# Moving the weight slots and the low halves by 16 to 64 bytes in a four-layer decoder trunk

## The reference

```
layer 0, 3:  q, f, v, g = split(h @ w_in, 4)          # w_in 1024 x 4096
             gated linear recurrence in chunks of 64, 8 heads of 128; RMS norm; * silu(g)
layer 1:     h @ w_in                                  # w_in 1024 x 10240
             three dilated-window attentions (128,1), (512,4), (2048,16), 16 heads of 64,
             QK norm and ALiBi, merged by their softmax denominators; * silu(g)
layer 2:     u, v, g = split(h @ w_in, 3)              # w_in 1024 x 3072
             y = gelu(u) * (causal 128x128 mix of layer_norm(gelu(v)) + b_s) * silu(g)
every layer: x = x + y @ w_out                         # w_out 1024 x 1024
```

## Time and profile before

| | |
|---|---|
| median of 3 runs | 1348.52 us (1348.16 to 1348.88) |
| span of the profiled execution | 1346.8 us; the 1.7 us to the median lie around it |
| PE busy | 1339.1 us, 99% |
| PE weight loads busy | 1118.0 us, 83% (beside the matmuls) |
| DVE / ACT / POOL busy | 923.1 us / 687.2 us / 145.3 us |
| HBM traffic | 83 GB/s over the span |

### The profile page before, as it was taken

One profiled execution on the slowest core, in us unless ns is written; L12 is line 12 of the kernel. 1 busy time (PEld: TensorE's weight loads), 2 busy tenths in 40 slices (PEclk: granted clock), 3 DMA queues, 4 the chain that ended last, 5 costly groups with the idle time before them and its releaser, 6 DMA issues.

```text
span 1346.8 us, 22178 instructions
## 1 busy us (share of the span) xinstructions
PE 1339.1 (99%) x8759; PEld 1118.0 (83%) x8759; DVE 923.1 (69%) x1659; ACT 687.2 (51%) x1226; POOL 145.3 (11%) x224
## 2 busy tenths in 40 slices
PE   9999999999999999999999999999999999999999
PEld 8888888888888888888888887788888888888887
DVE  7867778564767576666676676865657577777782
ACT  6445555353655565656565656553434335454550
POOL 2422333000000000000000000000000022332220
DMA  6322233423222222222223131332333322232221
GB/s 194 95 80 79 64 94 95 118 79 91 66 79 79 79 79 79 79 79 79 79 68 90 48 92 50 105 93 71 94 94 94 110 76 83 63 93 76 84 64 63
DMA packets 211688, 113.62 MB, mean 84 GB/s; under 512 B 3743, under 2 KB 209889, under 8 KB 211586
## 3 DMA queue, kind: packets, MB, share of 16 engines
q1 hardware_dynamic: 211202, 112.02, 28.9%
q0 software_dynamic: 384, 0.20, 0.1%
HBM read 110.10 MB, written 2.10 MB: 83 GB/s over the span
## 4 chain that ended last, share of the span: by engine, by line
PE 96%; DVE 2%; ACT 1%; issue 1%; DMA 0%; SPq 0%; ACTq 0%; DVEq 0%
PE ps L647 39%; PE ps L662 38%; PE scores L662 4%; PE ps L1088 2%; PE ps L1072 2%; PE ps L1028 2%; PE ps L881 1%; PE scores L1056 1%; PE ps L1056 1%; PE scores L852 1%; PE ps L676 1%; PE ps L883 1%; PE scores L870 1%; PE scores L819 1%; PE ps L892 1%
## 5 line engine op out<-in xcount | busy, mean ns | idle before, releaser
L647 PE MATMUL ps<-op_hi,w_hi 128*128 128x512 f32 (+1 forms) x800 | 311.7, 390 | 0.0
L647 PE MATMUL ps<-op_lo,w_hi 128*128 128x512 f32 (+1 forms) x800 | 305.4, 382 | 0.0
L647 PE MATMUL ps<-op_hi,w_lo 128*128 128x512 f32 (+1 forms) x800 | 304.5, 381 | 0.0
L662 PE MATMUL ps<-w_hi,op_hi 128*128 128x512 f32 (+1 forms) x728 | 294.0, 404 | 1.6 <-DVE op_lo L1844 1.6
L662 PE MATMUL ps<-w_lo,op_hi 128*128 128x512 f32 (+1 forms) x728 | 282.6, 388 | 0.0
L662 PE MATMUL ps<-w_hi,op_lo 128*128 128x512 f32 (+1 forms) x728 | 282.2, 388 | 0.0
L1786 DVE TENSOR_TENSOR w_lo<-raw,w_hi 128x1024 fp32r<-128x1024 f32 x200 | 245.1, 1251 | 12.4 <-ACT w_hi L1274 10.9
L1274 ACT ACTIVATE w_hi<-raw 128x1024 fp32r<-128x1024 f32 x200 | 203.0, 1052 | 26.8 <-PE ps L662 11.2
L647 PEld LDWEIGHTS ps<-op_lo,w_hi 128*128 128x128 f32 x800 | 150.4, 188 | 29.9
L647 PEld LDWEIGHTS ps<-op_hi,w_hi 128*128 128x128 f32 x800 | 150.5, 188 | 27.4 <-DVE op_lo L1829 0.2
L647 PEld LDWEIGHTS ps<-op_hi,w_lo 128*128 128x128 f32 x800 | 150.7, 188 | 27.0
(11 more groups left out here) (228 smaller groups left out, 1944.9 us busy)
## 6 DMA issues: line engine op xcount, KB each, us to landing
raw<-in_b_w_in SPq DMA_DIRECT2D x80, 512.0 KB, 3.9
raw<-in_a_w_in SPq DMA_DIRECT2D x64, 512.0 KB, 4.2
raw<-in_c_w_in SPq DMA_DIRECT2D x24, 512.0 KB, 4.1
raw<-in_a_w_out SPq DMA_DIRECT2D x16, 512.0 KB, 4.3
raw<-in_b_w_out SPq DMA_DIRECT2D x8, 512.0 KB, 4.0
raw<-in_c_w_out SPq DMA_DIRECT2D x8, 512.0 KB, 4.9
xt<-in_x SPq DMA_DIRECT2D x4, 512.0 KB, 6.2
y<-in_norm_w SPq DMA_DIRECT2D x3, 512.0 KB, 4.7
```

The source lines that it names most:

```text
L647: last = nc.tensor.matmul(bank, a, b, start=(k == 0 and p == 0), stop=(k == KT - 1 and p == 2))
L662: last = nc.tensor.matmul(bank, a, b, start=(k == 0 and p == 0), stop=(k == KT - 1 and p == 2))
```

## The change

The same instructions are issued in the same order, with the same waits. Only addresses change. The row of `w_hi` for a slot gets 16 floats (64 bytes) more than it uses; `w_lo` and `op_lo` get 8 floats more and begin 4 floats (16 bytes) and 8 floats (32 bytes) behind their start. To make room, `vec_rows` loses its own 512 bytes and lies on the first tile of `a_sq` in `scratch`.

```diff
         op_hi = sb("op_hi", [P, KT, S], F32R)
-        op_lo = sb("op_lo", [P, KT, S], F32R)
+        op_lo = sb("op_lo", [P, 8 + KT * S], F32R)[:, 8:].rearrange("p (k c) -> p k c", k=KT)
         y = sb("y", [P, KT, S])
         raw = sb("raw", [P, RAW, KT, P])
-        w_hi = sb("w_hi", [P, SLOTS, KT, P], F32R)
-        w_lo = sb("w_lo", [P, SLOTS, KT, P], F32R)
+        w_hi = sb("w_hi", [P, SLOTS, KT * P + 16], F32R)[:, :, 0:KT * P].rearrange("p s (k c) -> p s k c", k=KT)
+        w_lo = sb("w_lo", [P, 8 + SLOTS * KT * P], F32R)[:, 4:4 + SLOTS * KT * P].rearrange(
+            "p (s k c) -> p s k c", s=SLOTS, k=KT)
...
-        vec_rows = sb("vec_rows", [40, P])
...
         a_sq, at = carve(at, TT, P)
+        vec_rows = a_sq[0:40, 0]
...
-                    nc.tensor.transpose(spare[:, 0:40], vec_rows[:], ident[0:40, 0:40]).then_inc(s_vecT, 1)
+                    nc.tensor.transpose(spare[:, 0:40], vec_rows, ident[0:40, 0:40]).then_inc(s_vecT, 1)
```

## The result

| | before | after |
|---|---|---|
| median | 1348.6 us | 1364.9 us (1364.3 to 1365.3) |
| ratio | | 1.012, 95% interval 1.0106 to 1.0134 |
| span of the profiled execution | 1346.8 us | 1363.1 us |
| PE busy | 1339.1 us | 1356.2 us |

The change made the kernel slower by 16.2 us. It was forecast 10 us faster; the range of 1316 to 1367 holds the time, on the side of the rivals.

The account below looks back on a forecast made before the run. PE, busy for 99% of the span, was taken as the bound through its matmul pace. 1528 steps x 6.67 ns gave 10.2 us less, other terms counted 0: 1348.5 to 1338.3 us, range 1316 to 1367.

Parts of the forecast that it names:

- every cover: Spare time beside PE for slower splits and `raw` DMAs, DVE's 31% idle and four `raw` slots, and no `vec_rows` wait: 0.
- Value taken: one unit less: Each of 1528 three-matmul steps on PE gets 16 clocks (6.67 ns) shorter: 10.2 us less in all; chance 0.27.
- they can be 32 + 24 + 24 = 80: Overhead clocks of a step's three 512-column matmuls after the change, against 96 clocks before.
- always sum to a multiple of 16: Rule claimed for the start overheads of a step's three matmuls on PE, in clocks of 2.4 GHz.
- the + 16 of `e_op` at 256 columns: Pace of 9 `e_op` matmuls, columns + 16 clocks; on every matmul 30.6 us less, one bound of the value.
- the rounding: Each PE matmul's start waits for the next instant that suits its addresses, instants being 16 clocks (6.67 ns) apart.
- the slower rival: Only the feature form is rounded up once more, 32 + 40 + 40 = 112 clocks: 4.9 us, 1353; chance 0.13.
- I take the value near zero: Choice of 10.2 us less between bounds of 30.6 us less and 30.6 us more for PE's matmuls.
- slower, by collision of weight load and moving operand: Slots' padding puts load and moving operand 64 bytes apart, columns + 48 clocks; on all matmuls 1379; chance 0.21, full or half.
- its half case: Collision of weight load and moving operand on half of the matmuls: 1364; chance 0.21 together with the full case.
- The rival of "nothing": `e_op`'s pace differs for another reason than its address; PE's pace stays 226.7 ns and the time 1348.5; chance 0.12.
- The settling phase: Uneven PE starts after short blocks, 0.23 us per group of 33, 16 groups in the chain; 0 taken, ±3.7 us.

## Why the prediction was wrong

The ground of the prediction stood: PE's pace is all that can move, it depends on where the operands lie, and every cover held (splits, `raw`, `vec_rows`). What failed is the step "Value taken: one unit less", and in it two things.

First, "they can be 32 + 24 + 24 = 80" took the 32 clocks of overhead as a need of at most 24, rounded up. With all offsets 0 no width from 240 columns on has less than 24.6, and no pair of offsets at 512 columns is under 32 (128 pairs; of the 1024 combinations of three none is under 96). Nowhere in what was measured was there slack to give back. The rule behind it, that the overheads of a step "always sum to a multiple of 16", fails too: steps settle at 132 and 136 clocks. The bound I took, the + 16 of `e_op` at 256 columns, was a steady pace of another width and did not carry over. It is not even a value of the addresses alone: in the kernel with only `op_lo` moved, `e_op`, `w_hi` and `w_lo` keep their places modulo 512, and the same steps take 117.8 ns (9 matmuls from 287.76 to 288.82 us) where they took 113.3.

Second, the rounding took the address of the moving operand alone. The runs show that the address of the weight load counts with it. The 32 bytes of `op_lo` alone slowed the token form, where `op_lo` is only loaded: 11.20 us for 48, + 48 clocks. The price of a moved part was not one unit more or less: the feature step of the change settles at 131 clocks where I had 80, and 112 in the slower rival.

The choice of a value between two ends ("I take the value near zero") fixed the sign. With + 16 and + 48 as ends, and the trace's uneven steps after short blocks (0.22 to 0.24 us, at the worst some 20 clocks above the steady pace), the kernel before's steady 32 looked like a middle. It was the lowest value that any pair of offsets had at 512 columns. A layout with unequal distances is a draw from a map whose median step is at 128 to 133 clocks, against 96.

The rival "slower, by collision of weight load and moving operand" named the right pair of reads and had 0.21; its half case gave 1364, and 1364.9 was measured. That match is luck: it was to come from the odd slots on half of the matmuls, and the slots alone do make 14 us, but `op_lo` or `w_lo` alone make more, and the three together less than either. Nor does its mechanism, a weight load in the way, show as such: the overhead does not shrink with the load. The rival of "nothing" is refuted: shifts by whole multiples of 16 bytes cost 14 to 22 us. Its grounds were the 16-byte lines of the page "SBUF — State Buffer" of the Trainium skill (Specifications), and lines alone do not account for these runs. The settling phase did not get shorter: the pieces of 33 went from 7.71 to 7.86 us. About half of the 0.23 us that the prediction put down to it is the very first step and no settling: in such a piece the second matmul starts 0.335 us after the first, which makes 0.11 us by itself.

What stays open is why. Instants at which PE may read, a bank pattern of 256 bytes, and a start that costs 28 clocks would fit together; no run shows any of the three by itself, and none explains why the same addresses gave 113.3 ns in one kernel and 117.8 in another. The state in which a stretch begins may count; it was not tested. Nor was a version found that beats the kernel before: its steady stretches are at the minimum that all maps show. Above it lie 4.5 us of uneven starts (up to 240 ns, summed over 227 ns) and 18.4 us in 200 matmuls that open a group after shorter ones, whose next start comes 306 to 341 ns later; the changed kernel has the same 200.

## What to carry to other kernels

Where PE takes weight loads and moving operands back to back, as here, their relative addresses are part of the pace, and equal offsets (here: all operands at the same place modulo 256 bytes, on a multiple of 32) can be the best and not the naive choice. Before moving anything, measure a map with a small kernel, since 64 pairs cost half a millisecond and told more than three variants of the whole kernel; but short stretches follow the map less well than long ones. And check an allocation change for what it does to addresses behind it: here 32 bytes in one operand cost 1.3%, and 16 bytes in all of them 1.1%.

## What the hardware showed that I had not expected

- Addresses matter in steps of 4 bytes and over a period of 256 bytes: 32 clocks at (0, 0) and (0, 28), 56 at (0, 4), 64 at (20, 4), 46 at (0, 128), 32 at (0, 256).
- The parts of a layout change do not add: 17, 14 and 22 us alone, 16 together.
- The overhead does not come from the weight load's length: 37 clocks with 16 weight columns, 32 with 128.
- In the kernel over the widths the starts of the stretches of 128 to 188 columns are 213.3 ns apart, and those of 196 to 236 columns 111.7 (8.62 and 4.53 us for 40). The clock changed between them, not the work. The trace's record of the granted clock begins only at 171.9 us, at 1.00, the 2.4 GHz level, and at that moment, inside the stretch of 192 columns, the distance falls from 213 to some 110 ns; so by its pace PE ran at the 1.2 GHz level for its first 153 us there, though it was busy all the time. The 1.00 that the profile's views print for earlier windows stands where there is no record. At either level the width made no difference in these stretches: 213.3 ns are 256 clocks of 1.2 GHz, 111.7 ns are 268 of 2.4 GHz.

```profile
102.41 8.62 PE ps L57 x40
...
174.02 4.53 PE ps L57 x40
```
